# Seven block products for eight in half of the projections of a two-branch decoder block

## The chip, the core and the metric

The kernel runs on one NeuronCore of one Trainium2 chip. The metric is the device time of one execution in microseconds (us). TensorE does the matrix products, ScalarE and VectorE the elementwise work, GpSimd very little so far, and SyncE issues the loads.

## What is computed

One pre-norm decoder layer on 512 tokens (plus 16 meta tokens) of width 1024, in float32. Cut to what matters:

```python
u = rmsnorm(h, norm_g)                                   # 528 x 1024
proj = einsum('bld,de->ble', u, w_in)                    # 1024 x 10240 weights
hq, hf, hi, hz, aq, ak, av, az, ga, gb = split(proj)     # ten of 1024 columns
f = lb + (1 - lb) * sigmoid(hf)                          # branch A, 8 heads
oA = merge_heads(rmsnorm(hgrn2_chunked(hq, log(f), 1 - f, hi)))
yA = einsum('blw,wd->bld', oA * silu(hz), w_branch_a)
oB = merge_heads(rmsnorm(diff_attention(rope(q), rope(k), v, lam)) * (1 - lam_init))
yB = einsum('blw,wd->bld', oB * silu(az), w_branch_b)    # branch B, 8 heads
m = sigmoid(ga) * yA + sigmoid(gb) * yB
out = rmsnorm(h + einsum('bld,de->ble', m, w_out), final_g)
```

## The kernel before, in words

All weights stream through SBUF in units of 1024 x 128 (one `w_raw` slot, 128 partitions x 1024 elements, of which there are two). To keep float32 accuracy, a unit is split: ScalarE copies it to the rounded type (`w_hi`, line 247), VectorE subtracts (`w_lo = w_raw - w_hi`, line 252), and TensorE adds three products into the same PSUM bank for each of the eight blocks of 128 rows (`three`, lines 385 to 387): high weight by high input, high by low, low by high. The input `u` is kept transposed and split the same way (`uT_hi`, `uT_lo`). Four units fit into the `w_hi` and `w_lo` ring. SyncE loads the next unit into a raw slot once VectorE has made the low part of the one in it.

There are 104 units: 64 in the head phase (8 for each of the 8 heads: HF, HQ, AK, AQ, HI, HZ, AV, AZ), 16 for the merge gates GA and GB, 16 for the two branch projections, 8 for the output. The order is written out by hand on each engine and held by semaphores. In TensorE's program a head is 64 slots; a slot is one block of 128 rows of one unit, and between slots stand the steps of the two token mixers (`HG_AT`, `AT_AT` say after which slot). Seven of them are the levels of the recurrence: TensorE multiplies (line 492 for the first, 506 for the others), VectorE scales `kk` and `qq` by products of `f` (lines 1096, 1097), copies a part to `sq` (1099) and merges the level into `aa` (1122); the next level's product waits for the copy. VectorE turns `kT` and `qT` by the rope table in between. GpSimd only raises small columns to the power -0.5, for the norms (371, 375, 378).

Of the kernel before, what the change touches and what calls it, by code (L numbers as in the profile page):

```python
# [26 lines left out]
P = 128  # L27
# [38 lines left out]
HG_AT = dict(zip(HG_STEPS, (3, 8, 11, 14, 17, 20, 23, 26, 30, 33, 36, 41)))  # L66
AT_AT = dict(zip(AT_STEPS, (23, 23, 30, 33, 33, 36, 38, 41, 43, 45, 47, 52, 54, 60)))
# [27 lines left out]
def build(nc, x, meta_tokens, norm_g, w_in, lb_logits, hg_norm_g, da_lambda, da_norm_g,  # L95
# [16 lines left out]

    w_raw, o = at("w_raw", [P, RAW, UNIT], F32, o)
    w_hi, o = at("w_hi", [P, SLOTS, UNIT], F32R, o)
    w_lo, o = at("w_lo", [P, SLOTS, UNIT], F32R, o)

# [4 lines left out]
    oa_hi, o = at("oa_hi", [P, KT, SEQ], F32R, region_o)  # L121
    oa_lo, o = at("oa_lo", [P, KT, SEQ], F32R, o)
    ob_hi, o = at("ob_hi", [P, KT, SEQ], F32R, o)
    ob_lo, o = at("ob_lo", [P, KT, SEQ], F32R, o)
    y_out, o3 = at("y_out", [P, CH, D], F32, region_o)
    y_sq, o3 = at("y_sq", [P, SEQ], F32, o3)

    ident, o = at("ident", [P, P], F32, o)
# [3 lines left out]
    small, o = at("small", [P, 128], F32, o)  # L132

    region_w = o
    f, o = at("f", [P, TOK], F32, o)
    tt, o = at("tt", [P, TOK], F32, o)
    q_1, o = at("q_1", [P, CH, P + P // 2], F32, o)
    aa, o = at("aa", [P, CH, P], F32, o)
    tg, _ = at("tg", [P, 4, SEQ], F32, region_w)
    region_m = o  # L140
    kk, o = at("kk", [P, TOK], F32, o)
    qq, o = at("qq", [P, SEQ], F32, o)
    k_tok, o = at("k_tok", [P, CH, P], F32, o)
    st, o = at("st", [P, CH, P], F32, o)
    sq, o = at("sq", [P, CH, P], F32, o)
    k_mix = sq[:, 0:CH // 2, :]
    on, o = at("on", [P, CH, P], F32, o)
    og, o = at("og", [P, SEQ], F32, o)
# [3 lines left out]
    kT, o = at("kT", [P, TOK], F32, o)  # L152
    qT, o = at("qT", [P, SEQ], F32, o)
# [5 lines left out]
    qT_lo, o = at("qT_lo", [P, SEQ], F32R, o)  # L159
    e1, o = at("e1", [P, 2, TOK], F32, o)  # L160
# [6 lines left out]
    lam_in, _ = at("lam_in", [P, 4, DA_D], F32, region_w)  # L167
    rows_in, _ = at("rows_in", [2 * HEADS + 2, P], F32, region_w + 4096)
    lam_pr, _ = at("lam_pr", [P, 2, DA_D], F32, region_w + 12288)
    m_hi, o2 = at("m_hi", [P, KT, SEQ], F32R, region_m)  # L170
    m_lo, o2 = at("m_lo", [P, KT, SEQ], F32R, o2)
    t_gate, o2 = at("t_gate", [P, 2, SEQ], F32, o2)
    t_m, o2 = at("t_m", [P, 2, SEQ], F32, o2)

    x_res, o3 = at("x_res", [P, CH, D], F32, base)
    g_fin, o3 = at("g_fin", [P, D], F32, o3)
# [26 lines left out]
    def level_bank(e):  # L203
# [9 lines left out]
    w_loaded = [sem(f"w_loaded{i}") for i in range(RAW)]  # L213

    slot_free = sem("slot_free")
    hi_ready, lo_ready, w_used = sem("hi_ready"), sem("lo_ready"), sem("w_used")
# [13 lines left out]
    o_squared, ms_ready, rstd_ready, on_ready, og_ready, oghi_ready, oglo_ready = (sem(n) for n in (  # L230
        "o_squared", "ms_ready", "rstd_ready", "on_ready", "og_ready", "oghi_ready", "oglo_ready"))
# [4 lines left out]
    gate_taken, y_taken, m_sum, mhi_ready, mlo_ready = (sem(n) for n in (  # L236
        "gate_taken", "y_taken", "m_sum", "mhi_ready", "mlo_ready"))
# [4 lines left out]
    def convert_hi(act, u, slot, loads):  # L242

        act.wait_ge(w_loaded[slot % RAW], 16 * loads)
        if not isinstance(u, int) or u >= SLOTS:
            act.wait_ge(w_used, u - SLOTS + 1)
        act.activation(w_hi[:, slot, :], w_raw[:, slot % RAW, :], ACT.Copy).then_inc(hi_ready, 1)  # L247

    def convert_lo(eng, u, slot):

        eng.wait_ge(hi_ready, u + 1)
        eng.tensor_tensor(w_lo[:, slot, :], w_raw[:, slot % RAW, :], w_hi[:, slot, :].bitcast(F32),  # L252
                          ALU.subtract).then_inc(lo_ready, 1)
# [35 lines left out]
    with block:  # L289

        @block.sync
        def _(sp):
# [14 lines left out]
            for i in range(CH):  # L307
                sp.dma_start(x_in[:, i, :], x[i * P:(i + 1) * P, :]).then_inc(x_loaded[i], 16)
                if i == 1:
                    section(0, 0, 0, 0)  # L310
# [1067 lines left out]
```

## Time and profile before

| | us |
|---|---|
| median of 3 runs | 753.86 (753.75 to 753.97) |
| the profiled execution, its own time | 753.44 |
| its span in the profile | 751.7 |
| TensorE busy | 731.2 |
| VectorE busy | 453.1 |
| ScalarE busy | 281.0 |
| GpSimd busy | 23.0 |

The span is the time that the trace covers; 1.7 us of the profiled execution lie around it. Busy times of matrix products overlap each other, since they are pipelined: what one costs is read from the distance between the starts of neighbours.

### The profile page before, as it was taken

The page shows a single profiled execution, that of the slowest core. Times are in us where ns is not written, and L with a number is a line of the kernel's source. Part 1 is how long each engine was busy: PE and PEld are TensorE (multiplying, and loading weights), DVE is VectorE, ACT ScalarE, POOL GpSimd, SP SyncE. Part 2 cuts the span into 40 slices and gives each one's busy share as a digit, 9 for nine tenths or more (in the row PEclk, how much of TensorE's full clock was granted, in tenths as well). Part 3 has the DMA queues.
Part 4 walks back from the last instruction along what each step waited for, and adds up shares of the span by engine and source line. Part 5 has one row for each costly group of instructions (what it writes and reads, how often), then busy time and mean ns, then how long its engine had stood idle before and what let it go on. Part 6 is the DMA issues. An engine that isn't in the chain of part 4 may idle for free.

```text
span 751.7 us, 12966 instructions
## 1 busy us (share of the span) xinstructions
PE 731.2 (97%) x4665; PEld 653.9 (87%) x4665; DVE 453.1 (60%) x1019; ACT 281.0 (37%) x548; POOL 23.0 (3%) x34
## 2 busy tenths in 40 slices
PE   2999999999999999999999999999999999999996
PEld 2998999999899899999989989998888888888885
DVE  4567569568667856956866785695643333233342
ACT  5414442642552444264155235425423222232232
POOL 2000000000000000000000000000000000000000
PEclk9899999999999999999999999999999999999999
DMA  7421220230122132023012213302323323323603
GB/s 265 122 76 57 86 84 12 72 112 28 56 87 81 50 90 84 2 82 112 28 56 84 84 35 104 85 1 85 112 85 112 95 87 98 112 84 98 237 29 113
DMA packets 105416, 63.44 MB, mean 84 GB/s; under 512 B 2066, under 2 KB 100772, under 8 KB 105396
## 3 DMA queue, kind: packets, MB, share of 16 engines
q1 hardware_dynamic: 105076, 62.52, 27.5%
q10 hardware_dynamic: 320, 0.66, 0.3%
q8 instruction: 12, 0.20, 0.1%
q14 instruction: 8, 0.07, 0.0%
HBM read 61.07 MB, written 2.10 MB: 84 GB/s over the span
## 4 chain that ended last, share of the span: by engine, by line
PE 96%; SPq 1%; issue 1%; DMA 1%; DVE 0%; ACT 0%; POOLq 0%; POOL 0%; DVEq 0%; ACTq 0%
PE ps L385 26%; PE ps L386 26%; PE ps L387 26%; PE ps L506 3%; PE ps L576 2%; PE ps L602 2%; PE ps L492 1%; PE ps L593 1%; PE ps L603 1%; PE ps L540 1%; PE ps L539 1%; PE ps L547 1%; PE ps L522 1%; DMA rows_in<-in_da_norm_g 1%; PE ps L531 1%
## 5 line engine op out<-in xcount | busy, mean ns | idle before, releaser
L385 PE MATMUL ps<-uT_hi,w_hi 128*128 128x512 f32 (+3 forms) x960 | 321.6, 335 | 0.0
L386 PE MATMUL ps<-uT_lo,w_hi 128*128 128x512 f32 (+3 forms) x960 | 308.7, 322 | 0.0
L387 PE MATMUL ps<-uT_hi,w_lo 128*128 128x512 f32 (+3 forms) x960 | 307.9, 321 | 0.0
L385 PEld LDWEIGHTS ps<-uT_hi,w_hi 128*128 128x128 f32 x960 | 181.6, 189 | 16.4 <-issue 3.2
L252 DVE TENSOR_TENSOR w_lo<-w_raw,w_hi 128x1024 fp32r<-128x1024 f32 x104 | 127.1, 1222 | 109.9 <-ACT w_hi L247 108.9
L387 PEld LDWEIGHTS ps<-uT_hi,w_lo 128*128 128x128 f32 x960 | 181.1, 189 | 13.9
L386 PEld LDWEIGHTS ps<-uT_lo,w_hi 128*128 128x128 f32 x960 | 181.6, 189 | 11.6
L247 ACT ACTIVATE w_hi<-w_raw 128x1024 fp32r<-128x1024 f32 x104 | 109.4, 1052 | 87.5 <-PE ps L387 84.3
L808 ACT ACTIVATE e<-e,small 128x144 f32<-128x144 f32 (+3 forms) x64 | 36.1, 565 | 41.9 <-DVE small L1200 41.9
L375 POOL TENSOR_TENSOR small<-small 128x4 f32<-128x4 f32 x16 | 16.1, 1008 | 507.3 <-DVE small L1135 362.7
L1133 DVE TENSOR_REDUCE small<-sq 128x4 f32<-128x512 f32 x16 | 11.0, 686 | 33.3 <-ACT sq L800 33.3
L506 PE MATMUL ps<-qq,sq 128*128 128x128 f32 x192 | 29.9, 278 | 0.0
L506 PEld LDWEIGHTS ps<-qq,sq 128*128 128x128 f32 x192 | 27.1, 190 | 3.0
L1122 DVE COPY_PREDICATED aa<-masks,ps 128x256 f32<-128x256 uint8 x56 | 29.1, 519 | 0.0
L827 ACT ACTIVATE kT_hi<-kT 128x528 fp32r<-128x528 f32 x8 | 5.2, 646 | 57.4 <-DVE kT L1174 57.4
L816 ACT ACTIVATE pT<-ps 128x128 f32<-128x128 f32 (+3 forms) x32 | 13.8, 432 | 31.6 <-PE ps L596 31.6
L385 PE MATMUL ps<-oa_hi,w_hi 128*128 128x512 f32 x64 | 24.9, 390 | 0.0
L386 PE MATMUL ps<-oa_lo,w_hi 128*128 128x512 f32 x64 | 24.9, 389 | 0.0
L387 PE MATMUL ps<-oa_hi,w_lo 128*128 128x512 f32 x64 | 24.9, 389 | 0.0
L385 PE MATMUL ps<-ob_hi,w_hi 128*128 128x512 f32 x64 | 24.9, 389 | 0.0
L386 PE MATMUL ps<-ob_lo,w_hi 128*128 128x512 f32 x64 | 24.9, 389 | 0.0
L387 PE MATMUL ps<-ob_hi,w_lo 128*128 128x512 f32 x64 | 24.9, 389 | 0.0
(185 smaller groups left out, 993.4 us busy)
## 6 DMA issues: line engine op xcount, KB each, us to landing
w_raw<-in_w_in SPq DMA_DIRECT2D x80, 512.0 KB, 3.7
w_raw<-in_w_branch_a SPq DMA_DIRECT2D x8, 512.0 KB, 3.6
w_raw<-in_w_branch_b SPq DMA_DIRECT2D x8, 512.0 KB, 3.6
w_raw<-in_w_out SPq DMA_DIRECT2D x8, 512.0 KB, 3.8
x_in<-in_x SPq DMA_DIRECT2D x4, 512.0 KB, 7.8
x_res<-in_x SPq DMA_DIRECT2D x4, 512.0 KB, 6.4
out<-y_out SPq DMA_DIRECT2D x8, 256.0 KB, 2.3
rope<-in_c_rope SPq DMA_DIRECT2D x1, 528.0 KB, 6.0
```

What stands on the lines that cost most here:

```text
L247: act.activation(w_hi[:, slot, :], w_raw[:, slot % RAW, :], ACT.Copy).then_inc(hi_ready, 1)
L252: eng.tensor_tensor(w_lo[:, slot, :], w_raw[:, slot % RAW, :], w_hi[:, slot, :].bitcast(F32), ALU.subtract).then_inc(lo_ready, 1)
L375: pool.tensor_tensor(rstd[:, 0:CH], ms[:, 0:CH], half_neg[:, 0:CH], ALU.pow).then_inc(rstd_ready, 1)
L385: pe.matmul(dst, w[0], rhs[0], start=start, stop=False, skip_group_check=True)
L386: pe.matmul(dst, w[0], rhs[1], start=False, stop=False, skip_group_check=True)
L387: return pe.matmul(dst, w[1], rhs[0], start=False, stop=stop, skip_group_check=True)
L506: mm = pe.matmul(walk(dst, i * P // 2, (P, 2), (m, P // (2 * m)), (1, m)), k_mix[:, i, :], walk(qq[:, i * P:], m, (HALF - m, 2), (2 * m, P ...
L576: mm = pe.matmul(bank(B_S + comp)[:, at_s:at_s + n - at_k], q[half[comp], q_b], k[half[comp], at_k:n], start=i == 0 and b != 1, stop=i == ...
L602: pe.matmul(dst, pT[:, j, :], v_b[:, j, :], start=(j == 0), stop=False)
L808: act.activation(e, e, ACT.Exp, bias=nb[:, at_nb:at_nb + 1], scale=-1.0, accum_out=(l_1, l_2)[comp][:, b:b + 1]).then_inc(exp_done, 1)
L816: act.activation(pT[:, 0:b + 1, :].rearrange("p j q -> p (j q)"), bank(B_T)[:, 0:(b + 1) * P], ACT.Copy)
L1122: dve.copy_predicated(dst, mask, got).then_inc(lvl_taken, 1)
```

## The change

Two units of weights with the same input are taken as one matrix of 1024 x 256 and cut into 2 x 2 blocks of 512 x 128, the input into 2 x 2 blocks of 256 tokens x 512. Strassen's scheme (in Winograd's form) makes their product from seven block products in place of eight. This is done for HF with HQ and AK with AQ of heads 1 to 7, and for the eight pairs GA, GB of the merge gates (two of them stand in the last head's program). Head 0's units, HI, HZ, AV and AZ of all heads, the branch and the output projections stay whole. Around it:

- A head's program on TensorE has 60 slots: 32 for HI, HZ, AV and AZ, then 28 for two pairs of 7 products, each product in two halves of two row blocks. Each row block is still three matrix products, now 256 columns wide (272 for the two products that also carry the meta tokens).
- GpSimd makes the four sums of weight blocks of a pair (`sum_1` to `sum_4`, each 128 x 512) and most low parts: per head three whole units (HZ, AV, AZ) and 12 of the 14 blocks of the pairs. VectorE makes the other two and HI's, in halves. For the gates VectorE makes five of seven low parts, GpSimd two.
- ScalarE makes the high part of each block; it saves the first product (`save_p1`) and takes the first output block (`c_11`). VectorE combines the rest, five additions of 128 x 256 a pair (`comb_16`, `comb_u3`, `comb_22`, `comb_21`, `comb_12`), which need PSUM banks 0 to 2.
- The sums of input blocks (`t_raw`, four of 128 x 1024) are made once, at the start: 3 of the subtractions and additions and the four low parts on GpSimd, 7 additions and subtractions on VectorE, the high parts on ScalarE.
- Both loads of a pair stay in the two raw slots until its seven parts are split. The ring holds 8 half units. The gates have two more raw slots (`w_raw2`).
- The outputs of the heads stay unsplit until the gate phase (`oa`, `ob`); `split_hi` and `split_lo` are done there, two heads at a time. All gates now run before the first branch unit.

The core of the diff:

```diff
-    def convert_hi(act, u, slot, loads):
-        act.activation(w_hi[:, slot, :], w_raw[:, slot % RAW, :], ACT.Copy).then_inc(hi_ready, 1)
-    def convert_lo(eng, u, slot):
-        eng.tensor_tensor(w_lo[:, slot, :], w_raw[:, slot % RAW, :], w_hi[:, slot, :].bitcast(F32),
-                          ALU.subtract).then_inc(lo_ready, 1)
+    def part_hi(act, q, j, r, loads, i, free):
+        if j in SUM_OF:
+            act.wait_ge(sums, 4 * q + SUM_OF[j])
+        else:
+            act.wait_ge(w_loaded[r + 1 if j == 5 else r], 16 * loads)
+        act.wait_ge(w_used, free)
+        act.activation(blk(w_hi, i), part_src(r, j), ACT.Copy).then_inc(pair_hi, 1)
+    def part_lo(eng, q, j, r, i, ready):
+        eng.wait_ge(pair_hi, PARTS * q + j + 1)
+        eng.tensor_tensor(blk(w_lo, i), part_src(r, j), blk(w_hi, i).bitcast(F32), ALU.subtract).then_inc(ready, 1)
...
+                def pair(r, between):
+                    sum_1(0, loads)
+                    sum_3(0, loads)
+                    between()
+                    low(r, 0)
+                    sum_2(q, 0)
+                    for j in range(1, 4 if r == 1 else 5):
+                        low(r, j)
+                    if r == 1:
+                        pool.wait_ge(v_lo, 2 * h + 1)
+                    sum_4(q, 0)
+                    if r == 0:
+                        low(r, 5)
+                    low(r, 6)
+                unit_lo(pool, UNITS * h + UNITS + 2, 1, 1, av_lo)
+                unit_lo(pool, UNITS * h + UNITS + 3, 0, 2, av_lo)
+                unit_lo(pool, UNITS * h + UNITS + 4, 1, 3, av_lo)
+                pair(0, lambda: None)
+                pair(1, lambda: rstd_pow(2 * h + 1))
...
+            def part(q, j, half, i, lo_done, meta):
+                if half == 0:
+                    pe.wait_ge(*lo_done)
+                    if j == 3:
+                        pe.wait_ge(comb, 10 + 5 * q + 1)
+                    elif j == 4:
+                        pe.wait_ge(p1_saved, q + 1)
+                    elif j == 5:
+                        pe.wait_ge(comb, 10 + 5 * q + 2)
+                    elif j == 6:
+                        pe.wait_ge(comb, 10 + 5 * q + 3)
...
-                conv(5)
-                conv(6)
-                norm(1, B_A)
-                conv(7)
+                    opening(h + 1, mark, chain)
+                    half_lo(dve, 0, h + 1)
+                sum_u3(1)
+                out_22(1)
+                norm_sum(1)
+                if not last:
+                    half_lo(dve, 1, UNITS * h + UNITS + 5)
+                norm(1, B_A)
+                out_21(1)
```

Where this moves instructions, in three places. First GpSimd, from its first steps on; `small` are the statistics of the norms, `t_raw` and `t_lo` the sums of input blocks, and the last rows before the loop's end are those of a head. Before, this is the whole of its work in the head phase:

```order
L371 TENSOR_TENSOR small<-small 128x1 [waits x_ms] x2
L373 UNCONDITIONAL_BRANCH
L373 ISA
L375 TENSOR_TENSOR small<-small 128x4 [waits ms_ready]
L373 REGISTER_ALU
L373 COMPARE_AND_BRANCH
```

Now the start, and a head's first eight operations (units HZ, AV, AZ, then the first pair):

```order
L500 TENSOR_TENSOR t_raw<-uT_hi 128x1024 [waits u_ready_lo]
L503 TENSOR_TENSOR t_raw<-t_raw,uT_lo 128x1024 [waits t3_sum]
...
L304 TENSOR_TENSOR w_lo<-w_raw,w_hi 128x1024 [waits hi_ready]
L303 REGISTER_ALU
L304 TENSOR_TENSOR w_lo<-w_raw,w_hi 128x1024 [waits hi_ready]
L303 REGISTER_ALU
L304 TENSOR_TENSOR w_lo<-w_raw,w_hi 128x1024 [waits hi_ready]
L522 ISA
L523 TENSOR_TENSOR w_sum<-w_raw 128x512 [waits w_loaded1]
L530 TENSOR_TENSOR w_raw<-w_raw 128x512 [waits w_loaded0]
L331 ISA
L332 TENSOR_TENSOR w_lo<-w_raw,w_hi 128x512 [waits pair_hi]
```

From 2 operations of 4 columns a head GpSimd goes to 2 of 4 columns, 3 of 1024 and 20 of 512. Second VectorE, in a head, where the first branch's norm ends. Before:

```order
L1142 TENSOR_TENSOR on<-ps,small 128x512 [waits rstd_ready]
L251 REGISTER_ALU
L252 TENSOR_TENSOR w_lo<-w_raw,w_hi 128x1024 [waits hi_ready]
L1210 RECIPROCAL small<-small 128x1 [waits exp_done]
```

Now:

```order
L1417 ISA [waits w_used]
L1418 TENSOR_TENSOR u_68<-ps,p_67 128x256 [waits comb]
L1610 TENSOR_TENSOR st<-ps,small 128x512 [waits rstd_ready]
L1422 REGISTER_ALU
L1442 TENSOR_TENSOR q_71<-ps,u_68 128x2x128 [waits comb]
L1614 REGISTER_ALU
L1616 ISA [waits hg_done]
L1616 TENSOR_TENSOR oa<-ps,gate_a 128x512
L331 ISA
L332 TENSOR_TENSOR w_lo<-w_raw,w_hi 128x512 [waits pair_hi]
```

Whole units' low parts leave VectorE; additions from PSUM and two blocks' low parts come in. Third TensorE, at the first step of the recurrence in a head of the loop. Now it stands two slots after the head's first unit begins, and the loop's branch ahead of that unit:

```order
L813 MATMUL ps<-ident,st 128x128 [waits on_ready]
L813 MATMUL ps<-ident,st 128x128 x3
L912 REGISTER_ALU
L912 COMPARE_AND_BRANCH
L608 MATMUL ps<-uT_hi,w_hi 128x272 [waits comb,c11_taken,lo_ready]
L609 MATMUL ps<-uT_lo,w_hi 128x272
...
L758 MATMUL ps<-q_71,kk 128x192 [waits k_ready]
L758 MATMUL ps<-q_71,kk 128x192 x3
```

The unit in that place (HI) now waits for the additions of the pair before it (`comb`) and for ScalarE's copy (`c11_taken`); the distances between the levels in slots are those of before (5, 3, 3, 3, 3, 3).

## Rows read from the trace of the kernel before

**Rows 1.** The page: busy times by engine, and the chain that ended last.

```profile
PE 731.2 (97%) x4665; PEld 653.9 (87%) x4665; DVE 453.1 (60%) x1019; ACT 281.0 (37%) x548; POOL 23.0 (3%) x34
PE 96%; SPq 1%; issue 1%; DMA 1%; DVE 0%; ACT 0%; POOLq 0%; POOL 0%; DVEq 0%; ACTq 0%
```

**Rows 2.** Windows: one head, gates and branches; busy (count) by engine, PEclk, DMA.

```profile
299.55:362.43 62.88, 62.88 (x461) 58.33 (x460) 44.73 (x112) 25.80 (x55) 2.01 (x2) 1.00 0.23 67
570.00:700.00 130.00, 130.00 (x568) 106.39 (x567) 44.65 (x47) 34.41 (x42) 0.00 (x0) 1.00 0.35 105
```

**Rows 3.** Timeline of TensorE, head 4: start, duration, line, operation.

```profile
301.41 0.29 PE L385 MATMUL ps<-uT_hi,w_hi 128*128 128x272 f32 x1
301.78 0.28 PE L385 MATMUL ps<-uT_hi,w_hi 128*128 128x256 f32 x1
302.14 0.29 PE L385 MATMUL ps<-uT_hi,w_hi 128*128 128x272 f32 x1
...
305.45 0.39 PE L385 MATMUL ps<-uT_hi,w_hi 128*128 128x512 f32 x1
306.14 0.40 PE L385 MATMUL ps<-uT_hi,w_hi 128*128 128x512 f32 x1
...
310.51 0.28 PE L385 MATMUL ps<-uT_hi,w_hi 128*128 128x264 f32 x1
310.87 0.28 PE L385 MATMUL ps<-uT_hi,w_hi 128*128 128x264 f32 x1
```

**Rows 4.** Groups by line, shapes apart: busy, mean ns, idle before.

```profile
L252 DVE TENSOR_TENSOR w_lo<-w_raw,w_hi 128x1024 fp32r<-128x1024 f32 x104 | 127.1, 1222 | 109.9 <-ACT w_hi L247 108.9
L1179 DVE TENSOR_TENSOR qT_lo<-qT,qT_hi 128x512 fp32r<-128x512 f32 x8 | 5.4, 680 | 0.0
L827 ACT ACTIVATE qT_hi<-qT 128x512 fp32r<-128x512 f32 x8 | 5.1, 632 | 8.4 <-DVE qT L1174 8.4
```

**Rows 5.** Timeline of GpSimd: memsets, then powers of one and of four columns.

```profile
0.74 0.10 POOL L363 MEMSET small<- 128x5 f32 x1 [0.29 <-POOLq L1367]
0.78 0.20 POOL L365 MEMSET pT<- 128x128 f32 x1
...
8.61 1.57 POOL L371 TENSOR_TENSOR small<-small 128x1 f32<-128x1 f32 x1 [1.94 <-DVE small L977]
...
19.34 0.55 POOL L371 TENSOR_TENSOR small<-small 128x1 f32<-128x1 f32 x1 [3.98 <-DVE small L977]
...
335.27 1.01 POOL L375 TENSOR_TENSOR small<-small 128x4 f32<-128x4 f32 x1 [42.73 <-DVE small L1135]
```

**Rows 6.** Timeline of all engines at 8.4 us: VectorE.

```profile
8.48 1.29 DVE L970 SCALAR_TENSOR_TENSOR x_in<-x_in,small,g_in 128x1024 f32<-128x1024 f32 x1
```

**Rows 7.** Timeline, head 4, levels 4 and 5 of the recurrence.

```profile
308.84 0.29 DVE L1099 COPY sq<-kk 128x256 f32<-128x256 f32 x1
...
309.37 0.61 PE L506 MATMUL ps<-qq,sq 128*128 128x128 f32 x4
...
311.68 0.29 DVE L1099 COPY sq<-kk 128x256 f32<-128x256 f32 x1
...
312.03 0.71 PE L506 MATMUL ps<-qq,sq 128*128 128x128 f32 x4
```

**Rows 8.** Timeline of VectorE at the start, up to the first head.

```profile
31.29 1.23 DVE L252 TENSOR_TENSOR w_lo<-w_raw,w_hi 128x1024 fp32r<-128x1024 f32 x1
...
43.42 0.43 DVE L1220 TENSOR_TENSOR q<-q,f 128x256 f32<-128x256 f32 x1
```

**Rows 9.** The chain that ended last: the first step of head 0.

```profile
48.07 1.30 PE ps L492 x8
```

**Rows 10.** The page, loads: queue, count, size, us to landing.

```profile
w_raw<-in_w_in SPq DMA_DIRECT2D x80, 512.0 KB, 3.7
```

**Rows 11.** Timeline, head 4: last block of probabilities, and its turn.

```profile
347.72 0.77 DVE L1212 SCALAR_TENSOR_TENSOR e<-e,small,e 128x528 f32<-128x528 f32 x1
...
349.47 0.60 PE L593 MATMUL ps<-ident,e 128*128 128x128 f32 x4
```

More of the change, by code:

```diff
@@ L343, in _ @@
-            for c in range(4):
-                load(O0 + c, c, w_out[:, 2 * c:2 * c + 2, 0:512])
-            sp.wait_ge(w_used, O0 - 2)
-            for i in range(CH):
-                sp.dma_start(x_res[:, i, :], x[i * P:(i + 1) * P, :]).then_inc(xres_loaded, 16)
+            sp.wait_ge(lo_ready, 1)
+            columns(0, AK, 0)
+            sp.wait_ge(lo_ready, 2)
+            columns(0, AQ, 1)
+            sp.wait_ge(lo_ready, 3)
+            columns(0, HI, 0)
+            sp.wait_ge(lo_ready, 4)
@@ L353, in _ @@
+            for half in range(2):
+                for c in range(4):
+                    u = BRANCH_UNITS + 4 * half + c
+                    sp.wait_ge(lo_ready, UNITS + HEADS + u - 3)
+                    load(u % 4, w_out[:, 2 * c:2 * c + 2, 512 * half:512 * (half + 1)])
+                if half == 0:
+                    for i in range(CH):
+                        sp.dma_start(x_res[:, i, :], x[i * P:(i + 1) * P, :]).then_inc(xres_loaded, 16)
             for i in range(CH):
@@ new lines, in _ @@
+            with pool.Fori(0, HEADS - 1) as h:
+                head(h, False)
+            head(HEADS - 1, True)
+            for n in range(GATES):
+                q, r, i = 2 * HEADS + n, n % 2 * RAW, 6 + PARTS * n
+                loads = 35 + n // 2 if r == 0 else 1 + n // 2
+                if n > 0:
+                    pool.wait_ge(pair_lo, LOWS * HEADS + 2 * n - 1)
+                    sum_1(r, loads)
+                    sum_3(r, loads)
+                pool.wait_ge(gate_lo, 5 * n + 1)
+                sum_2(q, r)
+                part_lo(pool, q, 2, r, i + 2, pair_lo)
+                part_lo(pool, q, 3, r, i + 3, pair_lo)
+                pool.wait_ge(gate_lo, 5 * n + 3)
+                sum_4(q, r)
@@ L480, in _ @@
             half_section(1, 1)
-            for s in range(2, AHEAD):
-                groups(s, s, s, range(KT))
+            for s in range(2, UNITS):
+                pe.wait_ge(lo_ready, s + 1)
+                pe.wait_ge(sec_taken, s - 1)
+                section(s, s + 3 & 3, range(KT))
             def level(h, e):
@@ L677, in project @@
+            pe.wait_ge(y_taken, 2 * KT - 4)
             def project(j, c, t):
@@ L852, in head, with p_1, parts @@
+                def p_1(r):
+                    save_p1(2 * h + r, made(h, 2 * UNITS + PARTS * r))
+                def parts(r, *js):
+                    for j in js:
+                        part_of_head(h, r, j)
+                unit_hi(act, 0, UNITS * h + 4, 2, made(h - 1, 21))
+                unit_hi(act, 1, UNITS * h + 4, 3, made(h - 1, 15))
                 rotated_hi(h, 0)
-                period(1)
-                period(2)
+                take(h, 4)
+                parts(0, 0)
+                take(h, 5)
@@ L855, in head @@
                 rotated_hi(h, 1)
-                conv(0)
-                period(3)
+                parts(0, 1, 2)
+                take(h, 6)
+                parts(0, 3)
                 exps(h, 0)
-                conv(1)
                 exps(h, 1)
+                parts(0, 4)
                 act.wait_ge(hg_done, hg(h, "keys"))
```

890 lines of the change are left out of this document (606 added, 284 removed).

## The prediction

> **What bounds the kernel now.** I read the page first: TensorE is busy 97% of the span, and the chain that ended last is TensorE for 96% of it; VectorE stands at 60%, ScalarE at 37%, GpSimd at 3% [rows 1]. Then the windows: in a head (62.88 us) TensorE has no idle time, and neither in 130 us of gates and branches [rows 2]. So any column taken from TensorE shortens the run, and any wait given to it lengthens it. Last, the timeline for what a product costs, by distances between starts, since the durations overlap [rows 3]: three products of 272 columns take 0.37 us, three of 256 take 0.36, three of 264 take 0.36, three of 512 take 0.69.
>
> The sum is made against the profiled execution, 753.4 us (span 751.7 and 1.7 around it); the median of the runs is 0.4 above it.
>
> **What TensorE saves.** HF before: 8 row blocks of 0.73 (272 and 256 columns) = 5.85 us. HQ: 8 of 2 x 0.355 = 5.68. AK: 8 of 2 x 0.36 = 5.77. AQ, and each gate unit: 8 of 0.69 = 5.55. A block product has four row blocks: 4 x 0.355 = 1.42 us, or 4 x 0.37 = 1.49 for 272 columns. A pair is now 5 x 1.42 + 2 x 1.49 = 10.1 us, where it was 11.5 (HF, HQ) or 11.3 (AK, AQ): 1.4 and 1.2 us saved, 2.6 a head, 18.4 over the seven heads. A gate pair is 7 x 1.42 = 9.95 for 11.1: 1.17 saved, 9.4 over eight. Together 27.8, rounded 28: **725.5 us** if nothing waits. A weight load per product stays, and it hides at 256 columns: that is in the 0.355 already, since half of HF and all of HQ are 256 wide.
>
> **What the others take on, per head (62.9 us now, 60.3 after).**
> - ScalarE: 14 parts of 512 for 4 units of 1024. Nearest row 0.63 for 512 [rows 4]: 8.8 us for about 4.2. With 25.8 busy [rows 2] it ends near 30 of 60: hidden, save where one part stands in line (below).
> - VectorE: loses 8 low parts of 1.22 and two splits of 0.68, 11.1 us; gains 4 pieces of 0.68 and 10 additions of 256 columns, which lie between the copy of 256 (0.29) [rows 7] and 0.68 for 512 [rows 4]; I take 0.45. 11.1 out, 7.2 in: 41 of 60 us. The additions free the banks that later products need: product 3 waits for bank 1, product 5 again, product 6 for bank 2. Each has about one product (1.4 us) plus a mixer step of room, against 0.45: hidden, if VectorE is on time.
> - GpSimd: 3 operations of 1024 and 20 of 512 with two inputs. No row shows one. From below the VectorE price, 1.22 and 0.68. From above: a memset costs 0.1 more for 123 more columns [rows 5], 0.8 ns a column for one stream; three streams and the 0.4 that a power of one column has as its fixed part give 1.65 for 512 and 2.9 for 1024. I take the middle, 1.2 and 2.2: 24 + 6.6 + 2 powers of 1.0 [rows 5] = 33 us of 60; 20 and 44 at the bounds. It fits in all three, so GpSimd's sum does not bound; its lateness may.
>
> The Trainium skill (GPSIMD Engine Reference, section Performance versus the Vector engine) gives 4497 ns for 2048 float32 columns of such an operation; an estimate from it is 1.1 to 1.2 us for 512 and 2.3 for 1024, and the sum would be the same 33 us.
>
> **The two places where lateness shows.** First, the end of a head. GpSimd's power for the first norm is queued behind the sums of the second pair, and behind it stand low 0, sum 2, lows 1, 2, 3, sum 4; then ScalarE's part 6, then the last exponentials, then VectorE's probabilities, then TensorE's turn of the block. Today the probabilities end 0.98 us ahead of that turn (348.49 to 349.47) [rows 11], and I estimate 0.7 us more ahead of the exponentials: about 1.7 of room for seven GpSimd operations, so each may be 0.24 us dearer than 1.2. At the upper price they are 3.0 late: 1.3 us of stall a head. The loads (3.7 us [rows 10]) stay ahead: the second pair's come when the first is split, some 13 us before it is needed; HI's has about 4 us to spare.
>
> Second, the levels. TensorE's level 4 starts 0.24 us after VectorE's copy ends (309.13 to 309.37), level 5 0.06 (311.97 to 312.03) [rows 7]. The new program keeps these distances. Whatever holds VectorE there holds TensorE, one for one. And something may: at 8.61 GpSimd's power of one column took 1.57 us in place of 0.55 [rows 5]; VectorE was in an operation with two SBUF inputs until 9.77 [rows 6], and GpSimd ended 0.41 after that. GpSimd waited for the whole VectorE instruction. Whether VectorE waits for GpSimd in the same way no row shows. In the levels VectorE has some 15 us of two-input work, and GpSimd will run the low parts of AV and AZ and the first sums beside it.
>
> The Trainium skill (SBUF — State Buffer, section SBUF: two separate sides) says that GpSimd and a VectorE instruction with two SBUF inputs lock each other out for the full instruction, whichever comes second. The trace agrees for one direction (1.57 for 0.55 us). By it this change would end on the rival's side below; by the rows alone it ends near 725.5.
>
> **At the start** VectorE gets seven operations of 1.22 (8.5 us) ahead of the first head's `f`, `kk`, `q`. It came to `q` at 43.42 with waits on the way [rows 8]; now 31.29 + 9 x 1.22 + 1.1 + 0.4 = 43.8. The first level step, at 48.07 [rows 9], moves two or so slots forward, to 46.6. Room 2.8 us: no cost unless GpSimd's seven operations (15.4 us) hold VectorE. The gates' end and the output are as before.
>
> **Forecast: most of it is kept.** Price: 725.5, plus 1.2 us a head over 8 heads (part of a GpSimd operation now and then in front of a level, or the upper price at the head's end) = 735. Own range 728 to 748: 0.3 to 2.8 a head. For it: GpSimd's operations would wait at least as often as VectorE's, and VectorE has idle time after the levels. I give it 0.36.
>
> **Rival 1: nothing waits**, 725.5 (724 to 728). For it: all sums of busy time fit with 19 us to spare. Against it: the 0.06 and 0.24 us. 0.18.
>
> **Rival 2, the other side: GpSimd's instructions hold VectorE in the levels.** Each head: lows of AV and AZ, 2 x 2.2 = 4.4, of which 1.3 fall beside VectorE's one-input work and 0.6 into idle time and the 0.24: 2.5 late. Sum 1, sum 3, low 0, sum 2: 4.8, of which 1.2 and then about 1.0 of later room: 2.6. So 5.1 us a head, 41 over eight. The gates: GpSimd's six operations (7.2) and VectorE's five lows and half a split (4.0) exclude each other: 11.2 against 9.95, 1.2 over six: 7. The start: of 15.4 us some 11 ahead of the first step, less 2.8: 8. Sum 725.5 + 56 = 782. With three quarters of it 768, with half of it 754. It decides from 3 us a head with 3 at the start. For it: the 1.57 us row. Against: with both queues full each gets turns, so GpSimd, which has time, takes part of the wait. 0.38, centre 768, from 755.4 to 790.
>
> **Rival 3: a draw**, the same mechanism at half price: 752.4 to 755.4, which is the 0.2% that a measurement of this kernel can tell from no change. 0.05. What is left, 0.03, is faster between 748 and 752.
>
> **The numbers.** Faster 0.36 + 0.18 + 0.03 = 0.57, same 0.05, slower 0.38. The likeliest single case that I can price gives 735; Rival 2 is as likely in sum but spread over 35 us. The range takes in Rival 1 from 724 and Rival 2 up to 783, which leaves about 0.1 above and little below. That the change doesn't save columns is excluded: the 256-column pace is there [rows 3].
>
> **What would show it.** The heads' period: 60.3 if nothing waits, 61.5 by the forecast, over 63 by Rival 2. TensorE idle before the level steps, released by VectorE, with VectorE operations of 256 columns longer than their 0.43 while GpSimd is busy: Rival 2. GpSimd's operations of 512 over 1.65 us in the mean while VectorE's are as before: GpSimd takes the wait, as forecast. TensorE idle before the turn of probabilities in the second pair: the head's end. A gate pair at 9.95 us right, over 11.1 lost. The forecast is wrong if VectorE's two-input operations in the levels grow by over 3 us a head in sum.

## The result, and the profile after

The changed kernel takes 844.59 us (median of 4 runs, 843.99 to 848.97) beside 753.81 for the kernel before (4 runs): 1.122 times as long, 95% interval 1.118 to 1.126. The forecast was 735, the range ended at 783.

The page of the kernel after: span, busy time by engine, and from the slices TensorE's busy tenths and granted clock.

```profile
span 842.6 us, 14347 instructions
PE 742.1 (88%) x4953; PEld 671.4 (80%) x4953; DVE 586.1 (70%) x1113; ACT 324.7 (39%) x677; POOL 381.7 (45%) x261
PE   3867988899799899879979988997998999999997
PEclk9889999999899999999999999999999999999999
```

TensorE, 97% busy before [rows 1], is at 88%; GpSimd went from 23 to 382 us. What TensorE waited for (us in total, times, longest), without the wait for the input, which is as long in the kernel before (11.2 and 11.6 us):

```profile
PE ps L772 <- DVE sq L1564: 41.2, 22, 3.7
PE ps L608 <- DVE q L1442: 11.9, 8, 1.5
...
PE ps L769 <- DVE sq L1564: 7.2, 8, 0.9
PE ps L758 <- DVE q L1461: 6.8, 1, 6.8
PE ps L608 <- DVE u L1418: 4.4, 5, 1.9
PE ps L608 <- ACT kk L1037: 4.2, 1, 4.2
```

Five of the six are VectorE: the levels' copy `sq` (48.4 us), the combinations `q` and `u` (16.3), and the first head's `q` (6.8). The sixth is ScalarE's `kk` at the start; ScalarE itself had waited 4.2 us for one of VectorE's 8-column operations (L1365, shown below). What is left out is 2.0 us or less a line.

The first level's products, eight a head, from their group by source line (shortest, median and longest ns, first and last start):

```profile
L758 PE MATMUL ps<-q,kk x64: 324/326/689, 60.0 to 567.5; 128*128 128x192 f32 x64
```

The first of them stands at 60.0 where 46.6 was expected. The last is the eighth of head 7; that head's first stands at 566.4. So a head takes 506.4 / 7 = 72.3 us, where 62.88 stood before [rows 2] and 60.3 was the column sum. (The expectations below say 72.5 and 12.2 for 72.3 and 12.0: they count up to the eighth product.) The gate pairs are 11.1 us apart (GpSimd's `sum_2` at 646.95, 658.05, 669.18), as long as before; 9.95 was expected. The account is an estimate: 13.4 (start) + 8 x 12.0 (heads) + 6 x 1.2 (gates) = 117 on top of 725.5 is 842; the profiled execution took 844.9, so some 3 us have no term in it.

Of the 12.0 a head, 8.1 are the waits above (41.2 + 7.2 + 11.9 + 4.4 over 8). The rest is slower work: TensorE is busy for 64.2 us a head in the mean of the seven, and for 60.3 with the same products in the kernel `k12` below. Windows of head 4: length, then busy time (instructions) of TensorE, its weight loads, VectorE, ScalarE, GpSimd; then the granted clock.

```profile
275.20:346.80 71.60, 64.85 (x461) 59.34 (x461) 52.84 (x115) 27.77 (x65) 37.87 (x26) 0.95 0.21 59
285.00:290.00 5.00, 4.05 (x17) 3.74 (x18) 4.97 (x11) 1.73 (x4) 0.86 (x2) 0.66 0.60 174
290.00:295.00 5.00, 3.12 (x17) 2.38 (x16) 4.79 (x7) 0.00 (x0) 5.00 (x4) 1.00 0.00 0
```

The granted clock was 1.00 (the upper level, 2.4 GHz) in one of these stretches of 5 us and 0.66 in the other. The slow one lies behind a wait: TensorE had waited 2.29 us for `sq` until 285.95. 0.66 is a mean of the upper and the lower level (1.2 GHz). From 295 to 300, behind the next wait (1.88 us until 294.57), it is 0.66 again.

Why VectorE was late there, from the timelines of VectorE, GpSimd and TensorE (start, length, engine, line, operation, and in brackets the idle time before it):

```profile
280.78 2.40 DVE L1561 TENSOR_TENSOR kk<-kk,f 128x256 f32<-128x256 f32 x1
283.11 0.41 DVE L1562 TENSOR_TENSOR qq<-qq,f 128x256 f32<-128x256 f32 x1
283.44 2.45 DVE L1564 COPY sq<-kk 128x256 f32<-128x256 f32 x1
...
290.31 0.73 DVE L1622 STREAM_SHUFFLE e<-qT 128x512 f32<-128x512 f32 x1
...
291.73 1.50 DVE L1562 TENSOR_TENSOR qq<-qq,tt 128x256 f32<-128x256 f32 x1
293.16 1.35 DVE L1564 COPY sq<-kk 128x256 f32<-128x256 f32 x1
294.43 1.29 DVE L1570 TENSOR_TENSOR tt<-tt 128x64 f32<-128x64 f32 x1
295.65 0.43 DVE L1587 COPY_PREDICATED aa<-masks,ps 128x256 f32<-128x256 uint8 x1
```

```profile
280.17 2.73 POOL L304 TENSOR_TENSOR w_lo<-w_raw,w_hi 128x1024 fp32r<-128x1024 f32 x1 [2.25 <-ACT w_hi L299]
283.41 2.34 POOL L304 TENSOR_TENSOR w_lo<-w_raw,w_hi 128x1024 fp32r<-128x1024 f32 x1 [0.51 <-ACT w_hi L299]
...
291.49 1.47 POOL L530 TENSOR_TENSOR w_raw<-w_raw 128x512 f32<-128x512 f32 x1
292.92 1.44 POOL L332 TENSOR_TENSOR w_lo<-w_raw,w_hi 128x512 fp32r<-128x512 f32 x1
294.32 1.32 POOL L536 TENSOR_TENSOR w_raw<-w_sum,w_raw 128x512 f32<-128x512 f32 x1
```

```profile
285.95 1.22 PE L772 MATMUL ps<-qq,sq 128*128 128x128 f32 x4 [2.29 <-DVE sq L1564]
294.57 0.71 PE L772 MATMUL ps<-qq,sq 128*128 128x128 f32 x4 [1.88 <-DVE sq L1564]
```

`kk` and `sq` came just behind GpSimd's operations of 1024 and ended 0.3 and 0.1 us after them: 2.40 and 2.45 in place of 0.43 (the same shape in [rows 8]) and 0.29 [rows 7]. From 291 on the engines take turns: GpSimd has one operation of 512 after another, and between two of VectorE's operations one of them runs, so that even 64 columns take 1.29. Not every VectorE operation is held. `COPY_PREDICATED`, with an input in PSUM, keeps its 0.43, and `STREAM_SHUFFLE`, which reads one tile of SBUF, took 0.73 while GpSimd ran an operation from 289.88 to 291.53 (745 and 735 ns in the mean of the two groups of the run, 748 and 733 in `k12`). The groups say the same of the whole run (busy us, mean ns): `qq` and the copy doubled (419 and 287 ns before), the one with a PSUM input stayed (519 before).

```profile
L1562 DVE TENSOR_TENSOR qq<-qq,tt 128x256 f32<-128x256 f32 x40 | 34.1, 852 | 0.0
L1587 DVE COPY_PREDICATED aa<-masks,ps 128x256 f32<-128x256 uint8 x56 | 28.8, 515 | 0.0
L1564 DVE COPY sq<-kk 128x256 f32<-128x256 f32 x48 | 28.6, 596 | 0.0
```

At the start it is plainest: one operation of 128 columns (0.28 us before) and two of 8 (0.16 before), beside GpSimd's first sums of the input.

```profile
28.47 2.47 DVE L1358 TENSOR_TENSOR lam_pr<-lam_in 128x128 f32<-128x128 f32 x1
...
31.18 2.09 DVE L1362 TENSOR_TENSOR small<-small 128x8 f32<-128x8 f32 x1
...
33.39 2.31 DVE L1365 TENSOR_TENSOR small<-small 128x8 f32<-128x8 f32 x1
```

```profile
27.50 3.30 POOL L500 TENSOR_TENSOR t_raw<-uT_hi 128x1024 f32<-128x1024 f32 x1 [7.84 <-DVE uT_lo L1333]
30.88 2.38 POOL L503 TENSOR_TENSOR t_raw<-t_raw,uT_lo 128x1024 f32<-128x1024 f32 x1
33.33 2.35 POOL L505 TENSOR_TENSOR t_raw<-t_raw,uT_lo 128x1024 f32<-128x1024 f32 x1
```

### The profile page after: what moved, and what is told of

Read it like the earlier page. It is cut to its first block and busy times, and to the rows that moved or that the text cites. A ratio compares the mean times of both kernels' runs of the same rounds, so it can differ in the third digit from the quotient of the medians.

```text
span 842.6 us, 14347 instructions
## 1 busy us (share of the span) xinstructions
PE 742.1 (88%) x4953; PEld 671.4 (80%) x4953; DVE 586.1 (70%) x1113; ACT 324.7 (39%) x677; POOL 381.7 (45%) x261
## 5 line engine op out<-in xcount | busy, mean ns | idle before, releaser
L608 PE MATMUL ps<-uT_hi,w_hi 128*128 128x272 f32 (+3 forms) x704 | 233.4, 332 | 4.3 <-ACT kk L1037 4.2
L609 PE MATMUL ps<-uT_lo,w_hi 128*128 128x272 f32 (+3 forms) x704 | 221.9, 315 | 0.0
L610 PE MATMUL ps<-uT_hi,w_lo 128*128 128x272 f32 (+3 forms) x704 | 220.9, 314 | 0.0
L332 POOL TENSOR_TENSOR w_lo<-w_raw,w_hi 128x512 fp32r<-128x512 f32 x86 | 121.5, 1416 | 113.8 <-ACT w_hi L327 113.8
L608 PE MATMUL ps<-t_hi,w_hi 128*128 128x256 f32 x352 | 104.8, 298 | 17.3 <-DVE q L1442 11.9
L327 ACT ACTIVATE w_hi<-w_raw 128x512 fp32r<-128x512 f32 x132 | 79.0, 622 | 75.8 <-POOL w_raw L542 58.2
L610 PE MATMUL ps<-t_hi,w_lo 128*128 128x256 f32 x352 | 100.1, 284 | 0.0
L609 PE MATMUL ps<-t_lo,w_hi 128*128 128x256 f32 x352 | 100.0, 284 | 0.0
L608 PEld LDWEIGHTS ps<-t_hi,w_hi 128*128 128x128 f32 x352 | 67.6, 192 | 22.9 <-issue 15.3
L332 DVE TENSOR_TENSOR w_lo<-w_raw,w_hi 128x512 fp32r<-128x512 f32 x46 | 56.6, 1254 | 29.1 <-ACT w_hi L327 29.1
L304 DVE TENSOR_TENSOR w_lo<-w_raw,w_hi 128x1024 fp32r<-128x1024 f32 x29 | 35.3, 1223 | 54.6 <-ACT w_hi L299 54.6
L772 PE MATMUL ps<-qq,sq 128*128 128x128 f32 x192 | 35.5, 312 | 41.2 <-DVE sq L1564 41.2
L609 PEld LDWEIGHTS ps<-t_lo,w_hi 128*128 128x128 f32 x352 | 67.7, 192 | 0.0
```

Of the source, the lines that this page charges most:

```text
L304: eng.tensor_tensor(w_lo[:, slot, :], raw_at(r), w_hi[:, slot, :].bitcast(F32), ALU.subtract).then_inc(ready, 1)
L327: act.activation(blk(w_hi, i), part_src(r, j), ACT.Copy).then_inc(pair_hi, 1)
L332: eng.tensor_tensor(blk(w_lo, i), part_src(r, j), blk(w_hi, i).bitcast(F32), ALU.subtract).then_inc(ready, 1)
L608: pe.matmul(dst, w[0], rhs[0], start=start, stop=False, skip_group_check=True)
L609: pe.matmul(dst, w[0], rhs[1], start=False, stop=False, skip_group_check=True)
L610: return pe.matmul(dst, w[1], rhs[0], start=False, stop=stop, skip_group_check=True)
```

## The experiments

**Theory A**: GpSimd's operations and VectorE's operations on SBUF exclude each other for a whole instruction, whichever comes second; where TensorE waits for the VectorE operation that is held, TensorE pays, and pays again by the clock. **Rival B**: GpSimd's lateness (its chain, the loads that wait for it), the ring, or waits for banks. **Rival C**: the block products themselves cost more than by columns, or the clock falls by itself. "Period" is the distance from head 0's first level product to head 7's, over seven. Behind each time stands its ratio to the kernel before, measured beside it, with the 95% interval where it is near 1.

### GpSimd's work taken away, in whole or in part

`k1`: every GpSimd operation stays, one column wide:

```diff
-        eng.tensor_tensor(blk(w_lo, i), part_src(r, j), blk(w_hi, i)...
+        n = 1 if eng is pool_engine[0] else BLK
+        eng.tensor_tensor(blk(w_lo, i)[:, 0:n], part_src(r, j)[:, 0:n], blk(w_hi, i)[:, 0:n]...
```

> The changed kernel, in which every low part and every sum of weight blocks that GpSimd makes in the heads and the gates covers one column in place of 512 or 1024; the rest of these low parts and sums is left out (low parts stay zero or old). Order, waits, products and all of VectorE's and ScalarE's work stay, and so does GpSimd's work on the transposed input at the start. Theory A (GpSimd's operations with SBUF inputs hold VectorE's two-input operations, and TensorE's clock falls after the idle time): heads' period 60.3 to 61.5, gate pair 9.95 to 10.2, clock back over 0.99, and the whole 725.5 + 13 of the start = 738 (730 to 748). Rival B (bank waits on VectorE's additions, the ring of raw slots, the order of the queues): over 5 us a head of idle time stay, 790 or more. Rival C (products of 256 columns with their weight loads, or a power limit, cost the clock by themselves): the clock stays under 0.98 and the period over 65, 780 or more.

Measured 741.35 (0.984, interval 0.982 to 0.985): faster than the kernel before. Period 60.7, gate pair 10.02, and no wait at the levels is left. So 103 of the 119 us are the width of GpSimd's operations. `qq` and the copy are back at 419 and 286 ns. Rival C fell: with the same products a head takes nearly the column sum, and the mean clock rose from 0.967 to 0.984 (0.999 in `k12`, where the start is repaired too). What is left stands at the start: the first level product at 58.5, since the sums of the input were not cut.

`k3`: one column only for the three low parts of whole units.

> The changed kernel, in which only GpSimd's three low parts of whole units (HZ, AV, AZ, 1024 columns, one of them before and two within the levels) cover one column; the rest of these three low parts is left out. All sums and the pairs' low parts stay. Theory A with the hold in the levels by these three: half or more of the heads' excess of 12.2 us goes, 780 to 800, period 64.5 to 67. If it is the first pair's sums and low parts that hold the levels: period 69 to 72, 815 to 840. Rival B (end of a head): no more than 1 us a head, 836 or more.

Measured 813.76 (1.079), period 68.7: 30.8 us less. Time and period lie just under the second case of the expectation (815 to 840, 69 to 72), in which the first pair's sums and low parts hold the levels. The three operations of 1024 are some 7 of the 38 us that GpSimd is busy a head, and carry 3.9 of the cost (30.8 over eight); the 20 of 512 carry the rest, in the levels (`sq`, still 26.9 us of waits for 48.4) and before the combinations.

`k12`: `k1`, and the input's sums and low parts all on VectorE, one sum taken from another (13 operations for 14); a half of four of them stands in VectorE's wait for the last input tile, and the low parts stand behind the first head's opening.

> The changed kernel with GpSimd's low parts and sums in heads and gates one column wide (the rest of them left out), and the input's differences and their low parts made by VectorE, with no GpSimd work at the start. Theory A: all that GpSimd's operations cost is gone; the first level step at 46 to 48 in place of 58.5: 741.4 less 10 to 12, 727 to 733, which is the sum of the column count (725.5) and little more. If something else in the changed kernel costs (256-column products, clock, waits for banks): 738 or more.

Measured 729.78 (0.968, 0.967 to 0.970), the first level product at 46.3, period 60.7. A window over its second head (columns as above):

```profile
109.21:169.51 60.30, 60.30 (x460) 56.65 (x459) 40.32 (x116) 28.02 (x64) 8.05 (x25) 1.00 0.25 70
```

From the second head on a head takes the 60.3 of the column sum, without idle time of TensorE and at a clock of 1.00. The first takes 62.9, with 1.6 us of waits for `sq`, since VectorE's low parts of the input now stand ahead of its levels. With GpSimd out of the way the column sum is there to within 4.3 us, in a kernel that leaves out most low parts and sums but does every product.

### Reading or writing, late or held

`k2`: each operation replaced by three fills of its target, which read nothing:

```diff
+        for m in (n, n):
+            pool.memset(t[:, 0:m], 0.01).then_inc(fills, 1)
+            pool.wait_ge(fills, ...)
+        pool.memset(t[:, 0:n // 2], 0.01).then_inc(ready, 1)
```

> The changed kernel, in which each of GpSimd's low parts and sums in the heads and gates is replaced by three fills with a constant (full, full, half width) of the same target, which read nothing and take about as long (some 1.3 us for 512 columns, 2.4 for 1024), with the same waits and signals; GpSimd's loop over the heads is written out. Low parts and sums are left out. Theory A, with the inputs being what holds VectorE: as k1 with one column, 730 to 755. If GpSimd's writes hold VectorE as well, or if GpSimd's lateness (its chain at the head's end, the loads that wait for it) is the cause as rival B says: 820 to 850. Between them: both have a part.

Measured 775.28 (1.029): between. GpSimd was busy for 363 us, nearly as long as in the changed kernel, and the two-input operations were untouched; the copy was not:

```profile
L1587 DVE COPY sq<-kk 128x256 f32<-128x256 f32 x48 | 20.8, 433 | 0.0
...
L1585 DVE TENSOR_TENSOR qq<-qq,tt 128x256 f32<-128x256 f32 x40 | 16.7, 418 | 0.0
```

So 69 us go with the reading (844.6 to 775.3), and 34 with being late or with writing (775.3 to the 741.4 of `k1`). Here TensorE waits for `pT` (9.0 us), `e` (3.7) and `st` (3.3), the head's end that rival B named. Rival B has a part, of at most 34 of 103; how it splits between the copy and the lateness was not measured.

`k4`: the kernel before, with eight two-input GpSimd operations a head that nobody needs. `k4m`: fills in their place. In both, GpSimd's loop over the heads is written out and two tiles share memory, so what that costs is in `k4m` too.

```diff
+    pool.tensor_tensor(spare[:, :], bias[:, :], rope[:, 0, 0:512], ALU.subtract).then_inc(fills, 1)
```

> The kernel before, to which eight GpSimd operations of 512 columns with two SBUF inputs (constant tables) and an output that nobody reads are added in each head, two after each of the units HZ, AV, AZ and the one behind, so beside the levels; nobody waits for them. (Two tiles share memory to make room for the output.) Theory A: they hold VectorE's two-input operations, 10.3 us of GpSimd a head against 15 us of such work: 3 to 8 us a head and the clock falls in the windows of the levels, 775 to 820. If GpSimd takes the wait, as the forecast had it, or if a hold doesn't exist: 754 to 757.

> The kernel before with eight groups of three GpSimd fills a head (512, 512 and 256 columns, nobody reads them), at the places where the eight two-input operations stood, and about as long; GpSimd's loop over the heads is written out. Theory A, with SBUF inputs being what holds two-input operations, and writes holding only VectorE's copies from SBUF to SBUF: VectorE's operations kk and qq stay at 0.42, the copy of 256 columns grows from 0.29 to 0.4 to 0.6, and the whole is 755 to 765, where the two-input operations made 786. If any GpSimd access holds VectorE: 780 to 790. If only lateness of GpSimd counts: 754.

Measured 786.40 (1.043) and 756.34 (1.004, 1.002 to 1.005). The place was not the expected one: the high parts they wait for were ready early, so both sets ran at the head's end, behind GpSimd's power for the norm, beside the next head's opening. VectorE and GpSimd in `k4`, then in `k4m`:

```profile
240.91 0.68 DVE L1162 TENSOR_TENSOR og<-ps,gate_b 128x512 f32<-128x512 f32 x1
242.46 1.59 DVE L1170 TENSOR_TENSOR ob_lo<-og,ob_hi 128x512 f32 x1 [0.87 <-ACT ob_hi L846]
243.97 1.52 DVE L1231 TENSOR_SCALAR f<-kk,small 128x528 f32<-128x528 f32 x1
245.41 1.49 DVE L1232 TENSOR_SCALAR kk<-kk,small 128x528 f32<-128x528 f32 x1
246.94 1.37 DVE L1234 TENSOR_TENSOR q<-q,f 128x256 f32<-128x256 f32 x1
...
239.99 11.21 POOL L380 TENSOR_TENSOR spare<-bias,rope 128x512 f32<-128x512 f32 x7
```

```profile
234.07 0.69 DVE L1171 TENSOR_TENSOR ob_lo<-og,ob_hi 128x512 f32 x1 [0.87 <-ACT ob_hi L847]
234.93 0.90 DVE L1232 TENSOR_SCALAR f<-kk,small 128x528 f32<-128x528 f32 x1 [0.16 <-issue]
235.75 0.83 DVE L1233 TENSOR_SCALAR kk<-kk,small 128x528 f32<-128x528 f32 x1
...
230.40 12.60 POOL L381 MEMSET spare<- 128x512 f32 x24
```

Beside GpSimd's reads the SBUF operations of VectorE that are shown take 1.4 to 1.6; the one with a PSUM input keeps 0.68. Beside the fills the two-input one keeps 0.69, and only the one-input ones grow, 0.55 to 0.9. The same GpSimd time (11 to 13 us a head) costs 32 us or 3. The change itself is not in these kernels: the hold alone makes `k4` slower.

### Other orders of the same arithmetic

From here on every kernel computes all. `k8`: GpSimd starts when level 6 is stepped; VectorE makes the three unit low parts, and low parts 2 and 3 of the gates.

```diff
-                unit_lo(pool, UNITS * h + UNITS + 3, 0, 2, av_lo)
+                pool.wait_ge(lvl_ready, 7 * h + 6)
...
                 step_level(2)
+                unit_lo(dve, UNITS * h + UNITS + 3, 0, 2, av_lo)
```

> The changed kernel with the same arithmetic, in another order: the low parts of HZ, AV and AZ are made by VectorE (between the level steps), GpSimd's sums and low parts of a head start only when level 6 has been stepped, ScalarE's parts 1 and 2 of the first pair stand behind the first exponentials, the level products stand 2 to 4 slots later, and in the gates VectorE makes low parts 2 and 3 too. Theory A (the two engines' SBUF work excludes each other, and only where VectorE is in line it costs): heads' period 61 to 62.5 for 72.5, gate pair 10.0 to 10.4 for 11.1, start as in the changed kernel (+12), 742 to 762 in sum. If VectorE is now too full in the levels (three operations of 1.22 more), the period stays over 64: 770 or more. Rival B (the end of a head, queues): 71 or more, 820 or more.

> As the one before (GpSimd after the levels), and the differences of the input and their low parts are all made by VectorE: 13 operations instead of 14 (one sum is taken from another), four of them in VectorE's wait for the last input tile, the four low parts behind the first head's opening; GpSimd has no work there. Theory A: at the start VectorE's tiny operations (2.1 to 2.5 us beside GpSimd) go back to 0.2, the first level step comes at 48 to 51 in place of 58 to 60: 7 to 10 us less than the one before, 733 to 754. If the start is bound by the sum of the work and not by the hold: 0 to 3 less.

`k8` measured 838.22 (1.111), period 72.1: a plain miss. `k9`, with the start as in `k12`, 826.38 (1.096), the first level product at 46.7: 11.8 us less than `k8`, all of the start and slightly more than the 7 to 10 expected, but 72 us over the 754 that its expectation ended at. Levels 2 to 6 were clean in both (`kk`, `qq` at 425 and 419 ns in the mean). Level 7, beside which GpSimd's first sums now ran, was not:

```profile
L1553 DVE TENSOR_TENSOR kk<-kk,tt 128x256 f32<-128x256 f32 x8 | 11.8, 1480 | 18.4 <-PE ps L744 18.4
```

And TensorE's waits, here of `k9`, had moved; the wait for `aa` is that of level 7:

```profile
PE ps L769 <- ACT v_a L1105: 28.0, 8, 3.5
PE ps L760 <- ACT k_tok L1156: 14.0, 8, 1.8
PE ps L754 <- DVE aa L1582: 12.9, 8, 1.6
```

Theory A left out what stands behind the levels. GpSimd's 26 us of sums and low parts now all lay between level 6 and the head's end; ScalarE, whose parts wait for them, held `v_a` 3.5 us back behind part 6.

> Same arithmetic as the run with the start moved to VectorE (826.4). There TensorE waited 3.5 us a head for v_a and 1.7 for k_tok, both from ScalarE, whose queue stood behind weight parts that wait for GpSimd's sums, and 1.6 for level 7, whose two operations took 1.5 in place of 0.42 beside GpSimd. Now ScalarE copies k_tok and the values ahead of the parts 3 to 6, and the late level products stand 1 to 2 slots earlier. Theory A (a hold in the levels was replaced by queueing behind GpSimd's late sums): 5 to 7 us a head of the 72.1 go, and 1 to 3 more by the clock: period 63 to 66, 755 to 780 in sum. If the queue is not the cause (GpSimd's 28 us a head don't fit behind the levels): another wait takes its place, period 69 or more, 800 or more.

> As the run beside it (ScalarE's queue reordered), and the first pair's low part 0 is made by VectorE in its wait for the level 7 product, so that GpSimd's first sums of a head need 3.9 us in place of 5.2. Theory A: 0.5 to 2 us a head less than the run beside it, 745 to 775. If the place on VectorE is no gap: the same or up to 0.7 a head more.

`k10` 815.50 (1.082), period 70.8; `k11` 810.72 (1.076), 70.1. `v_a` was gone from the list, and in its place came 18.0 us for `st`, the first norm, whose power stood on GpSimd behind the second pair's sums (the chain that the prediction named), and 9.5 for `q`. `k10` is the second case of its expectation. `k11` gained the expected 0.6 a head, in a time 36 us over its range. GpSimd's work doesn't fit behind the levels: each order moved the wait.

`k13`: GpSimd makes the powers alone, VectorE all sums and low parts. `k14` and `k15`: only the order of the queues, with some level products one slot later, each time for the longest waits that the trace before it showed. For instance, VectorE in `k15` against `k13`:

```diff
-                half_lo(dve, 0, h + 1)
                 sum_u3(1)
                 out_22(1)
+                norm_sum(1)
...
+                half_lo(dve, 0, h + 1)
```

> The same arithmetic with no GpSimd work but the powers: all sums and low parts of heads, gates and start are made by VectorE, in its gaps behind the levels (the level products 2 to 4 slots later, the unit low parts between them), and ScalarE's queue in the order of need. VectorE's busy time a head grows from about 40 to about 56 of 60 us by 20 operations of 0.6 and three of 1.2. Theory A (not the arithmetic but the two engines' exclusion costs): nearly all of the columns saved is kept, period 61 to 63, gate pair 10.0 to 10.4, 732 to 755 in sum, faster than the kernel before more likely than not. If VectorE alone has no room for it (its chains then stand late one behind another): period over 64.5, 765 or more, slower than the kernel before.

> The same arithmetic as the run before with all sums and low parts on VectorE (790.2), in another order of the queues only. There TensorE waited, per head, 1.1 us for k_tok, 1.1 for v_a, 0.7 to 1.2 for the third sum of the second pair (its VectorE operation stood behind the low part of HI, which waits for a transfer), 0.7 for the first, 1.1 for levels; and 6.3 once, for the same reason, in the last head. Each of the waiting operations now stands ahead of the one that held its queue; level 5 and 6 stand one slot later. Theory A: these waits are queue order and nothing else; 3.5 to 5 us a head and 4 to 6 once: 740 to 760, period 62.5 to 64. If VectorE's load (about 56 of 61 us) is what holds, the waits come back at other places: 775 to 790.

> As the run before (771.1, all sums and low parts on VectorE), with the square and the sum for the second norm ahead of HI's parts on ScalarE and VectorE, and level 7 one slot later. TensorE waited there 2.1 us a head for the second turn and 0.8 for level 7, and the clock was at 0.98. Theory A (queue order alone): 2.5 to 3.5 us a head less, 743 to 752, period 62 to 63, just faster than the kernel before (753.6). If VectorE's load is the limit: the waits come back at another place, 760 to 771.

`k13` 790.18 (1.048), period 67.6: the second case of its expectation (over 765: VectorE alone has no room), but 20 us below the best with GpSimd, with VectorE at 76% of the span and none of `kk`, `qq` and the copy stretched (425, 420, 288 ns). The gate pairs are at 10.02. They are the place where the change paid first with its whole arithmetic: 10.5 already in `k8` to `k11`, where VectorE made all low parts of the gates and GpSimd only the sums, for 11.1 before. `k14` 771.12 (1.023), period 65.4, which misses its 760 by 11; `k15` 753.89 (1.0005, 0.9996 to 1.0014), period 63.2, level with the kernel before and 2 over the 752 that it was to stay under.

> As the run before (753.9), with ScalarE's copy of k_tok ahead of the second pair of exponentials, and in the last head the second norm ahead of the first gate's sums. TensorE waited there 1.0 us a head for k_tok, and 1.7 once for the norm. Theory A (queue order alone): 743 to 747, faster than the kernel before by about 1%. If VectorE's load is the limit: the waits come back elsewhere, 750 to 754.

> As the run before (753.0), with ScalarE's copies v_b and v_a ahead of weight part 5 of the first pair and its copy of the third turned probabilities ahead of parts 1 and 2 of the second. TensorE waited there 0.7 to 0.8 us a head for v_a and 0.3 to 0.4 for the probabilities. Theory A (queue order alone): 0.7 to 1.1 us a head less, 744 to 748, faster than the kernel before by 0.7 to 1.2%. If VectorE's load is the limit: less than 0.3 a head, 750.5 to 753.

`k16` 753.04 (0.9996): 0.9 less where 7 to 11 were expected; the wait for `k_tok` left, one of 0.7 for `v_a` came. `k17` (both ScalarE copies ahead of weight parts) 749.38 (0.9949, 0.9935 to 0.9963): faster than both kernels, by 0.5%, and 1.4 us over the 748 at which its expectation ended. Its page:

```profile
span 748.3 us, 14350 instructions
PE 717.2 (96%) x4953; PEld 652.4 (87%) x4953; DVE 597.2 (80%) x1343; ACT 322.6 (43%) x677; POOL 22.9 (3%) x34
```

TensorE's waits from 130 to 520 us, the heads behind the first (us in total, times, longest):

```profile
PE ps L696 <- DVE aa L1534: 1.7, 7, 0.3
PE ps L737 <- DVE st L1557: 1.0, 4, 0.4
```

No single wait there is over 0.4 us now, yet these heads take 62.3 against 60.3 in `k12` (the period is 62.8). In one head of `k16` the distances between starts put 0.8 of its 2.5 us at `v_a`, 0.4 at the third turned probabilities, 0.4 at a level, and the rest in smaller pieces. That VectorE's load (55 of 62 us a head, 40 in `k12`) costs those is likely but was not shown, and whether more queue order would win them back stays open.

## Why the prediction was wrong, step by step

- **"TensorE saves 28 us, 725.5 if nothing waits": right.** 729.8 in `k12`; gate pair 10.02 for 9.95, and 60.3 a head from the second on.
- **GpSimd's price, 1.2 and 2.2: right**, 1.29 for 512 and 2.37 for 1024 alone, inside the bounds.
- **"GpSimd, which has time, takes part of the wait": the step that failed.** The forecast put 1.2 us a head for it; 12.0 were measured. The exclusion is even-handed in form, an instruction each, but not in cost. GpSimd's instruction of 512 is three times as long as VectorE's of 256 (1.29 for 0.43), so a turn each means that VectorE pays up to 1.3 us per operation and GpSimd up to 0.4 (1416 ns in the mean for low parts that take 1290 alone). The sign that the prediction named came: `kk` and `qq` of levels 1 to 6 alone grew from 5.1 to 9.9 us a head, more than the 3 at which it called itself wrong. The 1.57 row [rows 5] had shown that a wait lasts for the partner's whole instruction; it showed this for GpSimd's side only, and for VectorE's side the forecast took no more than a part of a GpSimd operation now and then.
- **"5.1 us a head" of Rival 2: right mechanism, half the size.** 8.1 us of waits and 3.9 of slower work, so the time lies 55 us above that rival's own range too. Three terms were too small or missing. The 1.3 us "beside VectorE's one-input work" were counted as free, but copies and TENSOR_SCALAR are held as well (`sq` 287 to 596 ns). The waits before the combinations (`q`, `u`, 2.0 a head) were called hidden, with 1.4 us of room against 0.45; the combinations themselves, with PSUM inputs, kept their 0.41 to 0.43, but VectorE came late from its low parts of 512 (1254 ns in the mean over heads and gates, 690 in `k1`). And the clock behind each wait stood in no sum: in head 4 TensorE was busy for 64.85 us at a mean of 0.95, which is by estimate 61.6 at 1.00.
- **The start, "no cost unless GpSimd's operations hold VectorE": they did**, 13.4 where the rival had 8, since even 8-column operations cost 2.1 to 2.3. 6.8 of it is the wait for the first head's `q`, 4.2 the one for ScalarE's `kk`.
- **The gates: the rival's 7 us, measured 7** (1.2 over six), by its own sum of 11.2 for the two engines' exclusive work against 11.1 seen.
- **The head's end (room 1.7 us)**: hardly in line in the changed kernel (1.6 us for `pT` and 0.9 for `st` in the whole run), where TensorE was late anyway. In `k2` and `k10` it came up, as `pT` and `st`.
- **The chances**: 0.38 for the right side, and a range that ended 62 us short. The case that came had a row (1.57 us), which the prediction itself named, and was priced by what would overlap, not by what each instruction does to the one behind it.

The Trainium skill (SBUF — State Buffer, section SBUF: two separate sides) says what the runs then showed: the lock goes to whoever starts first, for the whole instruction; it takes in VectorE operations with two SBUF inputs only against a GpSimd operation that reads SBUF, and one-input operations in a two-port mode against either. `k4` and `k4m` agree: 1.59 and 0.69 for the same two-input operation, 1.52 and 0.90 for `f`, where 692 and 553 ns are the means of the same two groups in the kernel before. No trace here shows in which mode an operation ran.

## What to carry to other kernels

Before work is given to GpSimd, list VectorE's operations with two inputs in SBUF, its copies and its TENSOR_SCALARs from SBUF, as far as TensorE waits for them in the same stretch, and charge each of them one whole GpSimd instruction, not a share of it. Free beside GpSimd were here VectorE's operations with a PSUM input and its shuffles. A low busy share of the helper says nothing by itself: what counts is which VectorE operations run beside it. And a saving on the engine that bounds is worth what the next engine's queue order lets through: here 24 us were there, and the first whole kernel that got any of them needed VectorE for all of the new work and four rounds of reordering, each for the longest wait of the last trace.

## What had not been expected of the hardware

- Two full queues that exclude each other took turns one by one, long against short: a 64-column operation took 1.29, where 256 columns take 0.43 undisturbed; in `k4` seven GpSimd operations in a row took 11.2 us, 1.6 each for 1.29 alone, while VectorE's own went through between them.
- What holds depends on where GpSimd's operands are: fills, 12.6 us a head, cost 2.7 us in the whole run (756.3 for 753.7); reads of about the same length 32.
- TensorE's granted clock was 0.66 in a stretch of 5 us behind a wait of 2.3 us, 1.00 in the next. With the waits gone the mean over the run is 0.999 (`k12`), with them 0.967: about a third of the heads' loss (3.9 of 12.0 us) was not waiting but slower work.
